# The samples' small matmuls in a retention decoder: 72 columns of weights on one place, or 32 columns on four partition quarters in turn

## The reference, cut to what matters

```
S_new[b] = gamma_h * S[b] + outer(k[b], v[b])          # 128 x 128, one per sample
o[b]     = q[b] @ S_new[b]                             # 1 x 128
o        = (o - mean(o)) * rsqrt(var(o) + EPS)         # per head, over the 128 values
ret_out  = o * g_ret * silu(g_r)
```

## Time and profile before

| what | value |
|---|---|
| time, median of 3 runs | 1210.65 us (1210.05 to 1211.07) |
| the profiled execution | 1209.43 us, of it 1207.6 us span |
| PE busy | 1190.3 us (99%) |
| PE weight loads busy | 1185.7 us (98%) |
| DVE busy | 921.4 us (76%) |
| ACT busy | 605.7 us (50%) |
| POOL busy | 87.6 us (7%) |
| granted clock of PE | 1.0 |

### The profile page before, as it was taken

How to read it: one execution, slowest core, us unless ns; L and a number is a source line. 1 busy time by engine, 2 the same in 40 slices (tenths; PEclk the granted TensorE clock), 3 DMA queues, 4 the chain that set the end, 5 groups by cost and what they waited for, 6 DMA issues and landing times.

```text
span 1207.6 us, 25290 instructions
## 1 busy us (share of the span) xinstructions
PE 1190.3 (99%) x9804; PEld 1185.7 (98%) x9804; DVE 921.4 (76%) x1465; ACT 605.7 (50%) x917; POOL 87.6 (7%) x104
## 2 busy tenths in 40 slices
PE   6999999999999999999999999999999999999998
PEld 6999999999999999999999999999999999999998
DVE  6799799999986643588869979999999764346863
ACT  7333565555556444545444435555555554455341
POOL 0000000000010011201110000000000100121000
PEclk9999999999999999999999999999999999999999
DMA  8455755545555654424546565555555445543462
GB/s 306 173 209 197 215 204 187 192 177 194 192 180 173 238 181 174 175 91 155 209 175 216 202 205 200 203 184 185 186 207 203 162 174 216 196 148 138 144 212 100
DMA packets 43466, 225.80 MB, mean 187 GB/s; under 512 B 6401, under 2 KB 13057, under 8 KB 19585
## 3 DMA queue, kind: packets, MB, share of 16 engines
q1 hardware_dynamic: 29520, 200.14, 46.4%
q10 hardware_dynamic: 13872, 24.65, 6.3%
HBM read 210.97 MB, written 13.81 MB: 186 GB/s over the span
## 4 chain that ended last, share of the span: by engine, by line
PE 88%; DVE 5%; issue 3%; DMA 2%; ACT 2%; ACTq 1%; DVEq 0%; SPq 0%
PE accum_all L475 26%; PE accum_all L476 26%; PE accum_all L477 26%; PE ps L541 2%; DMA raw<-w_in 1%; PE accum_all L566 1%; DVE wlo L1088 1%; PE accum_all L567 1%; PE accum_all L568 1%; DVE tmp L1164 1%; ACT whi L719 1%; DVE c_buf L1164 1%; DMA pre<-w_in 1%; PE ps L491 1%; PE ps L516 1%
## 5 line engine op out<-in xcount | busy, mean ns | idle before, releaser
L475 PE MATMUL accum_all<-a_hi,whi 128*128 128x264 f32 x2048 | 585.2, 286 | 2.3 <-DVE wlo L1341 2.3
L476 PE MATMUL accum_all<-a_lo,whi 128*128 128x264 f32 x2048 | 580.3, 283 | 0.0
L477 PE MATMUL accum_all<-a_hi,wlo 128*128 128x264 f32 x2048 | 580.1, 283 | 0.0
L1088 DVE TENSOR_TENSOR wlo<-raw,whi 128x2048 fp32r<-128x2048 f32 x182 | 421.5, 2317 | 182.9 <-ACT whi L719 182.8
L719 ACT ACTIVATE whi<-raw 128x2048 fp32r<-128x2048 f32 x182 | 347.5, 1912 | 158.7 <-DMA raw<-w_in 85.7
L475 PEld LDWEIGHTS accum_all<-a_hi,whi 128*128 128x128 f32 x2048 | 385.8, 188 | 3.2 <-issue 2.5
L476 PEld LDWEIGHTS accum_all<-a_lo,whi 128*128 128x128 f32 x2048 | 386.1, 189 | 0.8
L477 PEld LDWEIGHTS accum_all<-a_hi,wlo 128*128 128x128 f32 x2048 | 384.1, 188 | 0.0
L475 PE MATMUL accum_all<-b_hi,whi 128*128 128x264 f32 x672 | 191.0, 284 | 0.0
L476 PE MATMUL accum_all<-b_lo,whi 128*128 128x264 f32 x672 | 190.4, 283 | 0.0
L477 PE MATMUL accum_all<-b_hi,wlo 128*128 128x264 f32 x672 | 190.3, 283 | 0.0
(11 more groups left out here) (213 smaller groups left out, 1260.8 us busy)
## 6 DMA issues: line engine op xcount, KB each, us to landing
raw<-w_in SPq DMA_DIRECT2D x108, 1024.0 KB, 4.8
raw<-w_out SPq DMA_DIRECT2D x32, 1024.0 KB, 4.8
raw<-w_gate SPq DMA_DIRECT2D x32, 1024.0 KB, 4.8
s_new<-s_ret ACTq DMA_DIRECT2D x16, 512.0 KB, 3.6
ss_out<-s_new ACTq DMA_DIRECT2D x16, 512.0 KB, 2.6
raw<-w_pw SPq DMA_DIRECT2D x8, 1024.0 KB, 4.8
x<-x_t SPq DMA_DIRECT2D x4, 528.0 KB, 7.7
raw<-w_in SPq DMA_DIRECT2D x8, 256.0 KB, 8.0
```

The costliest lines, as they stand in the source:

```text
L475: pe.matmul(accum[bank][:, 0:R], w_hi[:, w:w + P], hi, start=k == 0, stop=False)
L476: pe.matmul(accum[bank][:, 0:R], w_hi[:, w:w + P], lo, start=False, stop=False)
L477: mm = pe.matmul(accum[bank][:, 0:R], w_lo[:, w:w + P], hi, start=False, stop=k == k_tiles - 1)
L1088: v.tensor_tensor(wlo[:, slot, :], raw[:, side, :], whi[:, slot, :].bitcast(F32), ALU.subtract).then_inc(s.lo_ready, 1)
```

## The change

The eight products of `ret_samples` have 32 columns of weights instead of 72 (`QW = P // BANKS`, with `BANKS` 4), and product b writes to the partition quarter b mod 4: partitions 0, 32, 64, 96 on. Samples b and b+4 share a quarter, the first of them starts the accumulation. As sample b is still in column b of its block, it lands on partition 32 * (b mod 4) + b. The statistics, the normalisation by ACT and the turn go over all 128 rows of the block, POOL sets no zeros in `og`, and the gate is two instructions: one reads the eight samples from `ps_s0` by a stride of 33 (and 4 within a quarter), one does the 256 prompt rows.

```
-QW = 72
+QW = P // BANKS
...
             for b in range(DEC):
-                mm = pe.matmul(ps_s1[0:QW, 0:P], q_diag[:, b, :], s_new[:, b * P:(b + 1) * P], start=b == 0,
-                               stop=b == DEC - 1)
+                at = QW * (b % BANKS)
+                mm = pe.matmul(ps_s1[at:at + QW, 0:P], q_diag[:, b, :], s_new[:, b * P:(b + 1) * P], start=b < BANKS,
+                               stop=b >= BANKS)
...
-            nc.scalar.activation(og[0:DEC, 2, :], ps_s1[0:DEC, 0:P], ACT.Identity,
-                                 bias=nb_t[0:DEC, 2:3], scale=sc_t[0:DEC, 2:3]).then_inc(s.og_ready, 1)
+            nc.scalar.activation(og[:, 2, :], ps_s1[:, 0:P], ACT.Identity,
+                                 bias=nb_t[:, 2:3], scale=sc_t[:, 2:3]).then_inc(s.og_ready, 1)
...
-            v.bn_stats(bn[0:DEC, 12:18], ps_s1[0:DEC, 0:P]).then_inc(s.bn_done, 1)
+            v.bn_stats(bn[:, 12:18], ps_s1[:, 0:P]).then_inc(s.bn_done, 1)
...
-            v.bn_aggr(mv[0:DEC, 2, :], bn[0:DEC, 12:18]).then_inc(s.mv_ready, 1)
+            v.bn_aggr(mv[:, 2, :], bn[:, 12:18]).then_inc(s.mv_ready, 1)
...
-            v.scalar_tensor_tensor(rt[:, :], ps_s0[:, 0:R], vec(l, (h - 1) + V_RET), sg[:, :], ALU.mult,
+            turned = ps_s0[:, 2 * P:2 * P + BANKS * (QW + 1)].rearrange("p (j c) -> p j c", c=QW + 1)[:, :, 0:DEC:BANKS]
+            of_samples = lambda t: t[:, SEQ:R].rearrange("p (g j) -> p j g", j=BANKS)
+            v.scalar_tensor_tensor(of_samples(rt), turned, vec(l, (h - 1) + V_RET), of_samples(sg), ALU.mult, ALU.mult)
+            v.scalar_tensor_tensor(rt[:, 0:SEQ], ps_s0[:, 0:SEQ], vec(l, (h - 1) + V_RET), sg[:, 0:SEQ], ALU.mult,
                                    ALU.mult).then_inc(s.rt_ready, 1)
...
-            nc.gpsimd.memset(stack[:, :].bitcast(F32), 0.0)
-            nc.gpsimd.memset(og[:, 2, :], 0.0).then_inc(s.zeros_set, 1)
+            nc.gpsimd.memset(stack[:, :].bitcast(F32), 0.0).then_inc(s.zeros_set, 1)
```

## The result

The changed kernel takes 1194.26 us (median of 4 runs, 1193.03 to 1196.74) against 1210.35 us of the kernel before in the same comparison. The ratio is 0.9876 with a 95% interval of 0.9863 to 0.9889, a gain of 1.2%, 16.1 us.

The account below looks back on a forecast made before the run. PE's own stream was taken as the bound. Sixteen groups at 0.76 - 0.32 = 0.44 us save 7.0 us: span 1207.6 to 1200.6, time 1202.4, and 1203.6 us with the median's 1.2 added; range 1195 to 1217.

Parts of the forecast that it names:

- PE sets the end: PE, busy 1190.3 of 1207.6 us with 13.6 us of waits, passes savings to the time nearly one to one.
- the gain arrives whole: Other engines' rooms, the shortest 1.85 us, cover the shorter groups, so 0.44 us a group reaches the end.
- Fewer columns alone gain nothing: In the samples' matmuls, moving columns, not weight columns, set the 0.109 us between passes; these stay at 128.
- Quarters overlap: In the samples' matmuls, passes writing to different partition quarters can run at the same time; the trace before showed none.
- The number of steps: A group's eight products take 9 steps, 0.98 us in place of 1.75, gaining 0.76 us a group.
- The rival of four at once: Four passes of the samples overlap, 4 steps, no border price: 1.31 us a group gained, 1189.7 us; chance 0.04.
- The border: Between full matmuls and the samples' group, the array empties at each side: 2 x 0.16 = 0.32 us a group.
- The sum: Per group of samples on PE, 0.76 gained less 0.32 paid: 0.44 us net, 7.0 us for sixteen groups.
- The speed-up of 2.38: Skill's figure for three column tiles of long matmuls, applied to the samples: 1.0 us a group saved, about 1194 us.
- The other engines: DVE, ACT and POOL work stays hidden; DVE takes 0.08 to 0.17 us more a head, against 2.4 us idle.
- What is late next: With shorter samples' matmuls, the turn's wait for `og` has the shortest room, 1.85 us; at most 0.93 is used.
- wrong from the side: Sign against the forecast: a new PE wait, of the turn for `og` or of DVE's making; waits should stay unchanged.

Follow-up runs that it names:

- e1: Changed kernel with all eight 32-column products writing to the first partition quarter: 1213.42 us, ratio 1.0036 to the kernel before.
- e2: Changed kernel with the products alternating between the first two partition quarters: 1199.68 us, ratio 0.9926 to the kernel before.
- e3: Changed kernel with product order 0,4,1,5,2,6,3,7, two products of one quarter in succession: 1196.4 us, ratio 0.9891 to the kernel before.
- e5: Kernel before with everything of the change but the matmuls, which keep 72 columns at partition 0: 1208.74 us, ratio 1.0003.
- e10: Changed kernel without the products of samples 4 to 7, with DVE's statistics and ACT's normalisation earlier: 1197.93 us, ratio 0.9894 to the kernel before.

## Why the prediction came out as it did

**PE sets the end, and a saving there arrives.** Right in the main. The groups are 15.6 us shorter, about 14 of these reach the end in both profiles of the changed kernel, and the two comparisons of times gave 16.1 and 14.7 us. That the gain arrives whole was wrong by 1.5 to 1.7 us, by the new waits.

**Fewer columns alone gain nothing.** Right: e1 has 32 columns and 0.109 us between passes.

**Quarters overlap.** Right, and shown by e1, e2 and the changed kernel as a row: 1, 2 and 4 passes a step.

**The number of steps.** Wrong, and this is the step that failed. The prediction said that "the stream is in order", so the second pass of a product would hold back the next product, nine steps and a gain of 0.76 us a group. Measured were four steps: 0.37 us between first and last start where about 1.0 was forecast, and a gain of 1.29 us a group (0.975 net and 0.315 for the borders). The quarters do not wait for each other's order, which e3 shows with an order made to be the worst case for it. The rival of four at once had this right and was given 0.04, with the order of the passes as the argument against it. That starts keep this order across quarters was never seen in the trace; it was an assumption about how starts follow issue. In the kernel before, all passes shared the same columns, so it could show nothing of it. The second assumption of that rival, no border at all, was wrong by 5 us, so it too missed, at 1189.7.

**The border.** Right in size, but by luck. Taken was 2 x 0.16 = 0.32 us, for an array that must run empty while the next weights are loaded ahead as before. Measured were 0.12 in and 0.20 out, 0.32 in sum. But the weights are not loaded ahead on either side, and each border follows the duration of the load that stands there (0.106, 0.133 and 0.186 us of load, borders of 0.118, 0.144 and 0.198), not a constant 0.16. The transposes with 32 columns, which go in and out without a gap, did not speak for a product with 32 columns: e1 pays the border in the same quarter, with the same count of columns. By the rule of the Trainium skill, TensorEngine Tiling (Array Packing), section Tiling Modes, a change of mode drains the engine, and the runs agree for products with 32 and 64 columns: a load starts there only when the last matmul in flight is 0.07 us from its end. By the same rule the transposes with 32 columns, which pay nothing, did not change the mode here; that is inferred, and no run shows it or why.

**The sum.** 1.29 gained less 0.32 paid is 0.97 us a group; predicted were 0.76 - 0.32 = 0.44. The speed-up of 2.38 that the Trainium skill, TensorE: Matmul & The Clock Gate, section Part 3, gives for three column tiles, and that the prediction turned into some 1194 us, came out closest, by coincidence: it stands for three tiles and longer matmuls, and here the four quarters run at four passes a step, with the border as a term of its own, which together leave 0.975 of 1.870 us saved.

**The other engines.** Right for the change alone, e5 shows 1.0003. The statistics over 128 rows take 0.29 us against 0.28 for 8. The small gate instruction takes 0.22 us, more than the 0.17 taken:

```profile
L1241 DVE SCALAR_TENSOR_TENSOR rt<-ps,vecs,sg 128x256 f32<-128x256 f32 x16 | 7.6, 473 | 0.0
L1221 DVE BATCH_NORM_STATS2 small<-ps 128x6 f32<-128x128 f32 x16 | 4.6, 290 | 0.0
L1240 DVE SCALAR_TENSOR_TENSOR rt<-ps,vecs,sg 128x8 f32<-128x8 f32 x16 | 3.6, 224 | 0.0
```

**What is late next.** The turn's wait for `og` was named as the shortest room, 1.85 us, read in one head. That head was not the tightest: at the first turn of the two layers (167.95 and 761.37 us) the kernel before has 0.32 and 0.80 us of room, and there the changed kernel waits, 0.8 to 1.0 us in all. The new wait that the prediction named as a sign of being wrong from the side did come, and was small. The larger limit behind it, DVE at the end of the heads, was not named as a place, only as the bound that comes when the idle 2.4 us a head are used up. The average hides it: over six heads DVE has 1.4 us of idle time a head left, but in the last stretch of the heads it had none to speak of even before (0.2 of 18.3 us), and the changed kernel already stands at that limit.

## What to carry to other kernels

Products with few columns of weights can run beside each other when their outputs lie on different partition quarters; count the steps as the passes of the fullest quarter (both orders of issue tried here gave the same count), and add a border on each side of a group that stands between full matmuls, about the duration of the weight load that is made there. Put all such products into one group, since the border was the same for eight passes as for sixteen. When a trace has no row for an overlap, give the case of full overlap a real chance, and before shortening PE further look at how much idle time the next engine has at the end of a stage, not only within it, and read the room of a wait in every head, not in one.

## What the runs showed of the hardware

- Passes to different quarters start 7 ns apart when issued in turn, 13 to 14 ns apart when two products of a quarter are issued in succession, and overtake each other (e3).
- Within a quarter passes stand 0.109 us apart, as with the full array; the first distance in a group is 0.133 us (0.16 with 64 columns), and a burst of four is no slower than one pass.
- Going from full matmuls to products with 32 or 64 columns and back costs 0.12 and 0.20 us (0.14 and 0.20 with 64 columns), with one, two or four parts in use alike (the 64 columns were tried with two parts only). Weights are not loaded ahead across such a border, and each border costs the load's duration and some 0.012 us. With 72 columns it costs nothing, and transposes with 32 columns cost nothing either.
- Behind waits of 3.2 us (the changed kernel at 24.7 us, e10 at 339.1 us) PE's granted clock was 0.5 for 3.4 us, with 0.22 us between matmuls that stand 0.12 us apart at 1.0.
